# Gathering tokens for eight experts at a time in a mixture-of-experts stage, and loading the eleventh weight block in two transfers

## The chip, the cores and the metric

The kernel runs on one core of one Trainium2 chip. The time is the device time of one execution, in microseconds (us). The core has TensorE (PE, with its weight loads shown as PEld), VectorE (DVE), ScalarE (ACT), GpSimd (POOL) and SyncE (SP), which here only issues loads.

## What is computed

One inference step of a two-layer trunk for 128 context tokens and 128 latent tokens of width 1024, all in float32. Each layer has a mixer (a bidirectional mLSTM with 4 heads of 128, beside grouped-query attention with 8 query and 2 key heads of 64), and then the mixture of experts, the part that the change touches:

```
sel = softmax(xt @ w_router) + b_router            # 16 experts in 4 groups
grp = argmax over groups of (sum of the 2 largest sel in the group)
idx = the 2 largest sel inside that group;  w = scores[idx] / sum(scores[idx])
hid = silu(xt @ w_gate[e]) * (xt @ w_up[e])        # 1024 -> 512, per expert
y   = sum over e of gates[e] * (hid @ w_down[e])   # 512 -> 1024
x   = x + gate * y
```

The weights of one expert are three matrices of 2 MB each, so that one layer's experts are 96 MB (48 transfers of 2 MB), all of which are read.

## The kernel before

Tokens are held transposed, `xT` and `hT` as 8 blocks k of 128 features by 256 tokens. After the router a second copy `htok` holds them with tokens in the partitions, and `pick` (in the tile `lists`) holds for each expert and each of the two token sets (b = 0 context, b = 1 latent) a 0/1 matrix of 128 tokens by 32 places. A **gather** is a matmul of a block of `htok` with `pick`: its result in PSUM has 128 features by the places of several experts. ACT copies it into the tile `xe`, from where it is the stationary operand of the experts' first matmuls. A step for counts above 32 per expert exists, under a branch.

Experts go in 8 **pairs** p, and a quad q is two pairs. For pair p, PE runs `into_hidden(p, 0)` (gate: 16 matmuls of 512 columns) and `into_hidden(p, 1)` (up: 16 more), `turn_hidden` (4 transposes of `hid`, once DVE has made silu(gate) times up) and `down` (32 matmuls). In the even pairs from p = 2 a scatter of the quad before (`scatter_quad`, L1281) stands before and after `turn_hidden`; in pairs 1, 3 and 5 the gather of the next quad stands there: `gather(q + 1, 0, 1)` before `turn_hidden` and `gather(q + 1, 2, 3)` behind it. Pair 0 has `scatter_maps` and `clear_sums` there instead. A float32 matmul leaves two records, so 16 matmuls show as x32.

A quad's gather (L1220) has four PSUM banks, in each two feature blocks k and both b, that is 16 matmuls of 128 columns (4 experts times 32 places).

Weights: SP issues each 2 MB transfer in program order, into 10 **slots** during the experts (7 of the tile `ring`, 2 of `beside`, 1 of `over`). Per pair these are gate in two halves of the features (i = 0, 1), up in two halves (i = 2, 3), and down (i = 4, 5), one slot each. A slot is loaded again when its block has been read, by `expert_read`: i = 0 and 2 by `first_read`, a count that PE raises after the first 8 matmuls of gate or up; i = 1 and 3 when gate or up is done; i = 4 and 5 both when the pair's `down` is done. The transfers are numbered here from 0 within a layer: 0 to 9 go into slots that the mixer leaves, and number 10 (pair 1, i = 4) is the first that needs a slot read by the experts, namely number 0's. Numbers 14 and 15 (pair 2, both halves of up) need the down slots of pair 0. Of the last pair, down comes in halves of 1 MB.

```python
                        if last is not None:
                            was_read(last)
...
                            sp.dma_start(slot_space(slot).rearrange("p (k n) -> p k n", k=KF)[:, 0:n, :],
                                         w[l, 2 * p + i - 4, :, 0:n, :]).then_inc(slot_landed[slot], 16)
```

These are lines 618 to 637 of the program, and `into_hidden` is L1224 to L1240.

## Time and profile before

| | |
|---|---|
| median of 3 runs | 787.18 us (785.57, 787.18, 787.45) |
| the profiled execution | 786.11 us, its span 784.2 us |
| PE busy | 759.6 us, 97% of the span |
| PE weight loads | 410.0 us, 52% |
| DVE, ACT, POOL busy | 356.6, 160.4, 58.2 us |
| transfers | 289.45 MB, mean 369 GB/s |
| TensorE's granted clock, mean | 0.995 of full |

The expert stages are from 197 us (layer 0) and 570 us (layer 1) of the span, each to the next layer or the end. The profiled execution is 1.07 us below the median. In rows of the chain of waits the three fields are start, duration and the work; in rows of stretches each engine's busy time is followed by its count of instructions. Busy time of PE is modelled for pipelined matmuls, so a wait of PE on a transfer is read from the chain, where a DMA stands.

### The profile page before, as it was taken

How to read it: one execution, taken by the hardware profiler on the slowest of the kernel's cores; microseconds unless marked ns; L12 is line 12 of the kernel's file. 1: busy time of each engine (PE TensorE's matmuls, PEld its weight loads, DVE VectorE, ACT ScalarE, POOL GpSimd, SP SyncE). 2: the span in 40 equal slices, each digit the busy share in tenths (PEclk: the TensorE clock that was granted, in tenths of full speed). 3: DMA queues.
4: the chain of work that ended last, by engine and by line, in shares of the span. 5: the costliest groups of instructions: out<-in, count | busy, mean ns of one | idle time of the engine just before them, and what ended most of it. 6: DMA issues, size and time to landing. Idle time of an engine off the chain costs nothing.

```text
span 784.2 us, 11547 instructions
## 1 busy us (share of the span) xinstructions
PE 759.6 (97%) x4960; PEld 410.0 (52%) x4967; DVE 356.6 (45%) x560; ACT 160.4 (20%) x368; POOL 58.2 (7%) x70
## 2 busy tenths in 40 slices
PE   6999999999999999999899999999999999999987
PEld 5655646886434443444245546788643444344424
DVE  0206899786422232132248956788732223213222
ACT  3111224504112111120021111460411211112002
POOL 0410052001100000000010005200110000000000
PEclk8999999999999999999999999999999999999999
DMA  8999699898999999999999970679979999999993
GB/s 313 369 357 409 237 386 410 315 390 327 426 409 427 426 419 424 424 420 425 421 398 401 387 287 8 250 286 393 387 303 399 427 426 419 424 427 417 425 421 148
DMA packets 52980, 289.45 MB, mean 369 GB/s; under 512 B 3448, under 2 KB 5808, under 8 KB 27840
## 3 DMA queue, kind: packets, MB, share of 16 engines
q1 hardware_dynamic: 51200, 285.30, 90.4%
q0 software_dynamic: 1488, 3.31, 1.3%
q8 instruction: 41, 0.67, 0.3%
q10 hardware_dynamic: 240, 0.08, 0.0%
q14 instruction: 11, 0.09, 0.0%
HBM read 286.31 MB, written 2.37 MB: 368 GB/s over the span
## 4 chain that ended last, share of the span: by engine, by line
PE 77%; DMA 12%; DVE 5%; SPq 3%; issue 2%; ACT 1%; POOL 0%; DVEq 0%; ACTq 0%
PE ps L1236 23%; PE ps L879 12%; PE ps L1266 12%; PE ps L1150 7%; DMA ring<-in_w_e_up 5%; PE ps L1220 4%; DMA ring<-in_w_e_down 4%; DMA ring<-in_w_mod 3%; PE ps L897 3%; PE ps L1281 2%; SPq L635 1%; PE ps L727 1%; DVE pT L1860 1%; PE ps L1248 1%; PE ps L1028 1%
## 5 line engine op out<-in xcount | busy, mean ns | idle before, releaser
L1236 PE MATMUL ps<-ring,xe 128*64 128x512 f32 x688 | 151.6, 594 | 4.2 <-DMA ring<-in_w_e_up 4.2
L879 PE MATMUL ps<-ring,hT 128*128 128x512 f32 (+1 forms) x320 | 125.7, 551 | 0.0
L1236 PEld LDWEIGHTS ps<-ring,xe 128*64 128x64 f32 x688 | 48.6, 137 | 105.1 <-issue 100.6
L2205 DVE COPY ye<-ps 64x512 f32<-64x512 f32 (+1 forms) x28 | 19.3, 689 | 163.7 <-PE ps L1266 163.5
L1266 PE MATMUL ps<-ring,exhid 128*32 128x512 f32 x736 | 92.3, 594 | 0.8 <-DMA ring<-in_w_e_down 0.6
L879 PEld LDWEIGHTS ps<-ring,hT 128*128 128x128 f32 x320 | 60.1, 190 | 60.7 <-issue 58.4
L1150 PE MATMUL ps<-hT,ring 128*128 128x256 f32 x256 | 57.1, 381 | 0.0
L2189 DVE RECIPROCAL exhid<-exhid 128x512 f32<-128x512 f32 x16 | 53.6, 3353 | 0.5
L2187 DVE TENSOR_SCALAR exhid<-exhid 128x512 f32<-128x512 f32 x16 | 6.8, 427 | 103.2 <-ACT exhid L1678 103.2
L1266 PEld LDWEIGHTS ps<-ring,exhid 128*32 128x32 f32 x736 | 26.0, 110 | 53.0 <-issue 49.4
L1150 PEld LDWEIGHTS ps<-hT,ring 128*128 128x128 f32 x256 | 48.0, 190 | 7.4 <-issue 1.0
L1236 PE MATMUL ps<-beside,xe 128*64 128x512 f32 x208 | 46.2, 594 | 0.0
L1678 ACT ACTIVATE exhid<-ps 128x512 f32<-128x512 f32 x16 | 9.6, 597 | 144.1 <-PE ps L1236 144.1
L1266 PE MATMUL ps<-beside,exhid 128*32 128x512 f32 x224 | 35.3, 593 | 0.6 <-issue 0.6
L1220 PEld LDWEIGHTS ps<-lists,hT 128*128 128x128 f32 x256 | 29.7, 192 | 6.3 <-issue 6.3
L1220 PE MATMUL ps<-lists,hT 128*128 128x128 f32 x256 | 31.6, 278 | 0.5 <-ACT hT L1657 0.5
L1694 ACT ACTIVATE ye<-ps 64x512 f32<-64x512 f32 (+1 forms) x28 | 16.6, 592 | 68.2 <-PE ps L1266 68.1
L1236 PEld LDWEIGHTS ps<-beside,xe 128*64 128x64 f32 x208 | 14.6, 137 | 30.0 <-issue 29.9
L1671 ACT ACTIVATE xe<-ps 128x512 f32<-128x512 f32 x32 | 19.1, 597 | 54.0 <-PE ps L1220 54.0
L1236 PE MATMUL ps<-over,xe 128*64 128x512 f32 x128 | 28.9, 594 | 0.0
L897 PE MATMUL ps<-hT,ring 128*128 128x256 f32 x128 | 28.8, 381 | 0.0
L1860 DVE SCALAR_TENSOR_TENSOR pT<-ring,cT,pT 128x2048 f32<-128x2048 f32 x12 | 28.2, 2348 | 0.1
(294 smaller groups left out, 867.0 us busy)
## 6 DMA issues: line engine op xcount, KB each, us to landing
ring<-in_w_mod SPq DMA_DIRECT2D x24, 2048.0 KB, 16.8
ring<-in_w_e_up SPq DMA_DIRECT2D x23, 2048.0 KB, 19.9
ring<-in_w_e_gate SPq DMA_DIRECT2D x20, 2048.0 KB, 22.8
ring<-in_w_e_down SPq DMA_DIRECT2D x19, 2048.0 KB, 23.1
beside<-in_w_e_gate SPq DMA_DIRECT2D x8, 2048.0 KB, 22.1
ring<-in_w_in SPq DMA_DIRECT2D x7, 2048.0 KB, 20.4
beside<-in_w_e_down SPq DMA_DIRECT2D x7, 2048.0 KB, 20.3
beside<-in_w_e_up SPq DMA_DIRECT2D x5, 2048.0 KB, 18.6
```

The lines of the kernel that those rows point to most:

```text
L879: mm = pe.matmul(bank[:, 0:width], hT[:, k, b * P:(b + 1) * P], w[:, k, :], start=(k == 0), stop=(k == KD - 1))
L897: mm = pe.matmul(bank[:, j * TOK:(j + 1) * TOK], w[:, k, h * MD:(h + 1) * MD], hT[:, k, :], start=(k == 0 and len(ks) == KD), stop=(k == K ...
L1150: mm = pe.matmul(bank[:, j * TOK:(j + 1) * TOK], w[:, k, c:c + P], cat[:, k, :], start=(k == 0), stop=(k == KD - 1))
L1220: mm = pe.matmul(bank[:, c:c + P], htok[:, b, 2 * i + k, :], pick[:, b, 4 * q:4 * q + 4, :].rearrange("p e c -> p (e c)"), start=True, sto ...
L1236: mm = pe.matmul(bank[PLACES * j:PLACES * j + PLACES, :], xe[:, k, c:c + PLACES], w[:, j, i, :], start=(k == 0), stop=(k == KD - 1))
L1266: mm = pe.matmul(bank[32 * g:32 * g + 32, :], hidT[:, k, c:c + SLOTS], w[j][:, k, half * 512:(half + 1) * 512], start=(k == 0), stop=(k == ...
L1281: pe.matmul(sums(b, dj), ye[:, b, dj * P:(dj + 1) * P], scat[:, q, b * P:(b + 1) * P], start=False, stop=False, skip_group_check=True)
L1671: act.activation(xe[:, 2 * i:2 * i + 2, :].rearrange("p k (e b s) -> p b (k e) s", e=4, b=NB), bank[:, :].rearrange("p (b n s) -> p b n s" ...
L1694: ins = act.activation(ye[r, plane, 0:512], bank[r, :], ACT.Copy)
L1860: ins = dve.scalar_tensor_tensor(modsum[b], w[:, k % 2, :], one, modsum[b], ALU.mult, ALU.add)
L2189: dve.reciprocal(ex[:, :], ex[:, :]).then_inc(silu_step, 1)
L2205: ins = dve.tensor_copy(ye[r, plane, 512:1024], bank[r, :])
```

## The change

1. `gather(h, ...)` serves 8 experts, twice a layer (h = 0 before pair 0, h = 1 in pair 3). Each of its 8 banks holds one feature block k and both b: 2 matmuls of 256 columns. Pairs 1 and 5 have no gather.
2. Its result goes into two tiles, `xe` and the new `small` (8 x 256 floats per partition), by two copies of 256 elements per bank; ACT makes those of even k, DVE those of odd k. Pairs 0, 1, 4, 5 read `xe`, pairs 2, 3, 6, 7 `small`.
3. `small` shares its space with ten small tiles of the mixer (`C0`, `ck`, `cv`, `vx`, `rstd`, `qc`, `qk_r`, `peaks`, `hr`, `nst`). So ACT and DVE wait for `state_out` before the first copy, and two memsets of ones move from the start into each layer.
4. Transfer 10 is split: rows 0 and 2 of each partition once PE has read feature blocks 0 and 1 of gate (a new count `quarter_read`, after 4 matmuls), rows 1 and 3 after `first_read`. `down` of pair 1 waits for both.
5. Bank numbers: the first gather uses 0, 3, 4, 5; `count` goes from bank 5 to 6, ahead of it in DVE's order stand the copies.

```diff
-        put(("count", l), 5)
-        for i, bank in enumerate((0, 3, 1, 2)):
-            put((("gather", 0, i), l), bank)
+        for k in range(KD):
+            put((("gather", 0, k), l), (0, 3, 4, 5)[k % 4])
+        put(("count", l), 6)
...
-            if pair % 2 == 1 and pair < PAIRS - 1:
-                for i in range(4):
-                    put((("gather", pair // 2 + 1, i), l), i % 2)
+            if pair == PAIRS // 2 - 1:
+                for k in range(KD):
+                    put((("gather", 1, k), l), k % 2)
...
+                        if last == ("expert", l, 0, 0):
+                            rows = slot_space(slot).rearrange("p (k n) -> p k n", k=KF)
+                            sp.wait_ge(quarter_read, l + 1)
+                            sp.dma_start(rows[:, 0:KF:2, :], w[l, 2 * p + i - 4, :, 0:KF:2, :]).then_inc(even_rows, 16)
+                            was_read(last)
+                            sp.dma_start(rows[:, 1:KF:2, :], w[l, 2 * p + i - 4, :, 1:KF:2, :]).then_inc(slot_landed[slot], 16)
+                            continue
...
-                def gather(q, *which):
-
-                    for i in which:
-                        bank = begin((("gather", q, i), l))
-                        for k in range(2):
-                            for b in range(NB):
-                                c = b * TOK + k * P
-                                mm = pe.matmul(bank[:, c:c + P], htok[:, b, 2 * i + k, :],
-                                               pick[:, b, 4 * q:4 * q + 4, :].rearrange("p e c -> p (e c)"), start=True, stop=True)
-                        done((("gather", q, i), l), mm)
+                def gather(h, *which):
+
+                    for k in which:
+                        bank = begin((("gather", h, k), l))
+                        for b in range(NB):
+                            mm = pe.matmul(bank[:, b * 2 * P:(b + 1) * 2 * P], htok[:, b, k, :],
+                                           pick[:, b, 8 * h:8 * h + 8, :].rearrange("p e c -> p (e c)"), start=True, stop=True)
+                        done((("gather", h, k), l), mm)
...
-                            if p % 2 == 0 and u == 0 and k % 2 == 0:
-                                taken(pe, (("gather", p // 2, k // 2), l))
+                            if p % 4 == 0 and u == 0:
+                                taken(pe, (("gather", p // 4, k), l))
...
+                            if p == 0 and u == 0 and k == 1:
+                                mm.then_inc(quarter_read, 1)
...
+                    if p == 1:
+                        pe.wait_ge(even_rows, 16 * (l + 1))
...
-                    refill = p % 2 == 1 and q + 1 < QUADS
+                    refill = p == PAIRS // 2 - 1
...
-                        gather(q + 1, 0, 1)
+                        gather(1, 0, 1, 2, 3)
...
-                gather(0, 0, 1, 2, 3)
+                gather(0, *range(KD))
...
+                    for k in which:
+                        key = (("gather", h, k), l)
+                        bank = full(act, key)[:, :].rearrange("p (b q e s) -> p q b e s", b=NB, q=2, e=4)
+                        for q in range(2):
+                            ins = act.activation(places[q][:, k, :].rearrange("p (e b s) -> p b e s", e=4, b=NB), bank[:, q], ACT.Copy)
+                        ins.then_inc(free(key), 1)
...
-                pick_out(0, 0, 1, 2, 3)
+                act.wait_ge(state_out, 16 * STATE_OUTS * (l + 1))
+                pick_out(0, 0, 2, 4, 6)
...
-                chosen(0, 4).then_inc(pick_ready, 1)
+                chosen(0, 8).then_inc(pick_ready, 1)
...
+                dve.wait_ge(state_out, 16 * STATE_OUTS * (l + 1))
+                pick_out(0, 1, 3, 5, 7)
                 modulation_columns(*last_section(l))
```

PE's order from the first gather into pair 0 of layer 0, before (`lists` holds `pick`, `hT` holds `htok`, `rt,ones` is the count, `beside,xe` is gate):

```order
L1220 MATMUL ps<-lists,hT 128x128 [waits bank_read2,bank_read3,bank_read1,bank_read0,pick_ready]
L1220 MATMUL ps<-lists,hT 128x128 x3
L1220 MATMUL ps<-lists,hT 128x128 [waits bank_read3]
L1220 MATMUL ps<-lists,hT 128x128 x3
L1220 MATMUL ps<-lists,hT 128x128 [waits bank_read1]
L1220 MATMUL ps<-lists,hT 128x128 x3
L1220 MATMUL ps<-lists,hT 128x128 [waits bank_read2]
L1220 MATMUL ps<-lists,hT 128x128 x3
L1351 MATMUL ps<-rt,ones 128x16 [waits bank_read5]
L1351 MATMUL ps<-rt,ones 128x16
L1236 MATMUL ps<-beside,xe 64x512 [waits bank_read0,slot_landed7,bank_read1]
```

The same place in the changed kernel, from the fifth of the eight banks on (the first four read the same but for their banks):

```order
L1235 MATMUL ps<-lists,hT 128x256 [waits bank_read0]
L1235 MATMUL ps<-lists,hT 128x256
L1235 MATMUL ps<-lists,hT 128x256 [waits bank_read3]
L1235 MATMUL ps<-lists,hT 128x256
L1235 MATMUL ps<-lists,hT 128x256 [waits bank_read4]
L1235 MATMUL ps<-lists,hT 128x256
L1235 MATMUL ps<-lists,hT 128x256 [waits bank_read5]
L1235 MATMUL ps<-lists,hT 128x256
L1370 MATMUL ps<-rt,ones 128x16 [waits bank_read6]
L1370 MATMUL ps<-rt,ones 128x16
L1251 MATMUL ps<-beside,xe 64x512 [waits bank_read0,slot_landed7,bank_read1]
```

Ahead of pair 0 stand 16 matmuls in both, of 128 columns before and of 256 now.

PE's order in pair 1, from the end of `up` into `down`, before (`exhid` holds `hid`; L1248 is `turn_hidden`):

```order
L1236 MATMUL ps<-ring,xe 64x512 x7
L1220 MATMUL ps<-lists,hT 128x128 [waits bank_read0]
L1220 MATMUL ps<-lists,hT 128x128 x3
L1220 MATMUL ps<-lists,hT 128x128 [waits bank_read1]
L1220 MATMUL ps<-lists,hT 128x128 x3
L1248 MATMUL ps<-cst,exhid 128x128 [waits bank_read3,bank_read2]
L1248 MATMUL ps<-cst,exhid 128x128 x3
L1220 MATMUL ps<-lists,hT 128x128 [waits bank_read0]
L1220 MATMUL ps<-lists,hT 128x128 x3
L1220 MATMUL ps<-lists,hT 128x128 [waits bank_read1]
L1220 MATMUL ps<-lists,hT 128x128 x3
L1266 MATMUL ps<-beside,exhid 32x512 [waits bank_read3,slot_landed8,slot_landed7]
```

And now:

```order
L1251 MATMUL ps<-ring,xe 64x512 x7
L1265 MATMUL ps<-cst,exhid 128x128 [waits bank_read3,bank_read2]
L1265 MATMUL ps<-cst,exhid 128x128 x3
L1285 MATMUL ps<-beside,exhid 32x512 [waits bank_read3,even_rows,slot_landed8,slot_landed7]
L1285 MATMUL ps<-beside,exhid 32x512 x15
```

Nothing stands any more between `up` and `turn_hidden`, and between that and `down`.

SP's order at transfers 10 to 15 of layer 0, before:

```order
L635 DMA beside<-in_w_e_down 128x4096 [waits first_read]
L635 DMA beside<-in_w_e_down 128x4096 [waits bank_full1]
L630 DMA over<-in_w_e_gate 128x2x2048 [waits first_read]
L630 DMA ring<-in_w_e_gate 128x2x2048 [waits bank_full2]
L630 DMA ring<-in_w_e_up 128x2x2048 [waits bank_full2] x2
```

And now:

```order
L633 DMA beside<-in_w_e_down 128x2x1024 [waits quarter_read]
L635 DMA beside<-in_w_e_down 128x2x1024 [waits first_read]
L652 DMA beside<-in_w_e_down 128x4096 [waits bank_full1]
L647 DMA over<-in_w_e_gate 128x2x2048 [waits first_read]
L647 DMA ring<-in_w_e_gate 128x2x2048 [waits bank_full2]
L647 DMA ring<-in_w_e_up 128x2x2048 [waits bank_full2] x2
```

The first row became two; the waits of transfers 11 to 15 are the same.

## Rows read from the trace of the kernel before

**Rows 1.** The page: what the transfers moved, GB/s, in 40 slices of the span.

```profile
GB/s 313 369 357 409 237 386 410 315 390 327 426 409 427 426 419 424 424 420 425 421 398 401 387 287 8 250 286 393 387 303 399 427 426 419 424 427 417 425 421 148
```

**Rows 2.** Stretches: busy time of PE, PEld, DVE, ACT, POOL; PEclk, DMA share, GB/s.

```profile
601.00:770.00 169.00, 166.86 (x1094) 70.21 (x1094) 43.73 (x39) 21.70 (x37) 0.00 (x0) 1.00 1.00 420
760.00:764.00 4.00, 2.78 (x16) 0.96 (x16) 0.72 (x2) 0.00 (x0) 0.00 (x0) 1.00 1.00 418
```

**Rows 3.** The chain of waits, ends of both expert stages: start us, us, what.

```profile
351.07 0.67 SPq L630
351.78 37.76 DMA ring<-in_w_e_up
389.58 3.65 PE ps L1236 x16
...
743.39 28.59 DMA ring<-in_w_e_down
772.03 3.64 PE ps L1266 x32
```

**Rows 4.** The chain of waits, layer 1: gather, pair 0, start of pair 1.

```profile
569.62 3.81 PE ps L1220 x32
573.78 13.88 PE ps L1236 x64
...
590.63 7.07 PE ps L1266 x64
597.71 13.88 PE ps L1236 x64
611.59 1.98 PE ps L1220 x16
614.05 1.79 PE ps L1220 x16
```

**Rows 5.** Timeline of the SP queue: start us, us of a merged row, transfers.

```profile
204.88 3.77 SPq L635 DMA_DIRECT2D beside<-in_w_e_down  x2
...
225.38 0.88 SPq L630 DMA_DIRECT2D ring<-in_w_e_up  x2
...
577.41 0.34 SPq L635 DMA_DIRECT2D ring<-in_w_e_down  x1
...
597.76 0.88 SPq L630 DMA_DIRECT2D ring<-in_w_e_up  x2
```

**Rows 6.** Stretches in and around pair 0, columns as in rows 2.

```profile
577.50:599.20 21.70, 21.64 (x141) 8.12 (x140) 7.30 (x8) 3.14 (x6) 0.00 (x0) 1.00 0.96 387
227.00:228.00 1.00, 1.00 (x8) 0.40 (x6) 0.00 (x0) 0.00 (x0) 0.00 (x0) 1.00 0.83 303
577.00:578.00 1.00, 1.00 (x6) 0.29 (x4) 0.00 (x0) 0.00 (x0) 0.00 (x0) 1.00 0.00 0
578.00:579.00 1.00, 1.00 (x8) 0.38 (x6) 0.00 (x0) 0.00 (x0) 0.00 (x0) 1.00 1.33 229
599.00:600.00 1.00, 1.00 (x8) 0.41 (x6) 0.15 (x1) 0.00 (x0) 0.00 (x0) 1.00 0.59 172
```

**Rows 7.** The chain of waits, layer 0: gather and pair 0.

```profile
197.09 3.81 PE ps L1220 x32
201.25 13.88 PE ps L1236 x64
```

**Rows 8.** The chain of waits: 16 matmuls of 256 columns in layer 0.

```profile
160.78 6.91 PE ps L1150 x32
```

**Rows 9.** Groups by shape: busy us, mean ns of one, idle before.

```profile
L2196 DVE TENSOR_TENSOR exhid<-ps,exhid 128x512 f32<-128x512 f32 x16 | 11.1, 692 | 32.3 <-PE ps L1236 32.3
...
L1688 ACT ACTIVATE exhid<-ps 128x512 f32<-128x512 f32 x16 | 9.5, 595 | 75.3 <-PE ps L1248 75.3
...
L2023 DVE TENSOR_TENSOR qkr<-ps,shares 128x256 f32<-128x256 f32 x8 | 3.4, 425 | 0.3
...
L1624 ACT ACTIVATE qk<-ps 128x258 f32<-128x258 f32 x8 | 3.1, 387 | 1.4 <-PE ps L1120 1.1
```

More of the change, by code:

```diff
@@ L318, in build, with share @@
         m0 = sb("m0", [64, DEPTH, NB])
-        C0 = sb("C0", [P, 2 * MH, MD + 1])
-        ck = sb("ck", [P, NKV * HD])
-        cv = sb("cv", [P, NKV, HD + 1])
-        vx = sb("vx", [P, NB, NKV, HD + 1])
-        rstd = sb("rstd", [P, TOK])
-        qc = sb("qc", [P, NB, 4, 8])
-        qk_r = sb("qk_r", [P, NB, NQ + NKV])
-        peaks = sb("peaks", [P, NB, NQ])
+        small = sb("small", [P, KD * 4 * PLACES])
+        took = [0]
+        def share(n):
+            took[0] += n
+            return small[:, took[0] - n:took[0]]
+        C0 = share(2 * MH * (MD + 1)).rearrange("p (g e) -> p g e", g=2 * MH)
+        ck = share(NKV * HD)
+        cv = share(NKV * (HD + 1)).rearrange("p (g d) -> p g d", g=NKV)
+        vx = share(NB * NKV * (HD + 1)).rearrange("p (b g d) -> p b g d", b=NB, g=NKV)
+        rstd = share(TOK)
+        qc = share(NB * 4 * 8).rearrange("p (b q g) -> p b q g", b=NB, q=4)
+        qk_r = share(NB * (NQ + NKV)).rearrange("p (b h) -> p b h", b=NB)
+        peaks = share(NB * NQ).rearrange("p (b h) -> p b h", b=NB)
+        hr = share(NB * MH).rearrange("p (b h) -> p b h", b=NB)
+        nst = share(P)[0:8, :]
         shares = sb("shares", [P, NB, NQ])
         dn = sb("dn", [P, NB, MH, 2])
-        hr = sb("hr", [P, NB, MH])
-        nst = sb("nst", [8, P])
         mnew = sb("mnew", [64, DEPTH])
@@ L384, in build @@
         sq2 = xe
+        places = (xe, small[:, :].rearrange("p (k c) -> p k c", k=KD))
         h2 = lists
@@ L431, in build @@
         first_read, last_half = sem("first_read"), sem("last_half")
+        quarter_read, even_rows = sem("quarter_read"), sem("even_rows")
         front_in = [sem(f"{g}_front_in") for g in HALVED]
@@ L1210, in _ @@
                 token_rows(3)
[L1211 to L1222 removed]
+                warm((("gather", 0, 2), l), 3)
+                def gather(h, *which):
[5 more added lines that the diff above has]
+                        done((("gather", h, k), l), mm)
                 def into_hidden(p, u):
@@ L1339, in pair @@
                     if refill:
-                        gather(q + 1, 2, 3)
+                        gather(1, 4, 5, 6, 7)
                     if p == 0:
@@ L1665, in _, with pick_out @@
                 token_copy(3)
-                def pick_out(q, *which):
-                    for i in which:
-                        key = (("gather", q, i), l)
-                        bank = full(act, key)
-                        act.activation(xe[:, 2 * i:2 * i + 2, :].rearrange("p k (e b s) -> p b (k e) s", e=4, b=NB),
-                                       bank[:, :].rearrange("p (b n s) -> p b n s", b=NB, n=8), ACT.Copy).then_inc(free(key), 1)
+                def pick_out(h, *which):
+                    for k in which:
[4 more added lines that the diff above has]
+                        ins.then_inc(free(key), 1)
                 def pair(p):
-                    q, a = p // 2, p % 2
-                    refill = a == 1 and q + 1 < QUADS
+                    refill = p == PAIRS // 2 - 1
                     bank = full(act, (("gate", p), l))
@@ L1845, in _ @@
                 dve.memset(mv[:, :, :, MD:MD + 1], 1.0)
+                dve.memset(vx[:, :, :, HD:], 1.0)
+                dve.memset(cv[:, :, HD:], 1.0)
                 def section_sums(l, s, which):
@@ L2171, in _ @@
                 dve.tensor_copy(htok[:, 0, :, 64:128], bank[:, :].rearrange("p (k q) -> p k q", k=KD)).then_inc(free(key), 1)
-                chosen(4, E).then_inc(pick_ready, 1)
+                chosen(8, E).then_inc(pick_ready, 1)
                 step(dve.tensor_tensor(r(R_W), r(R_E), r(R_MASK), ALU.mult))
@@ L2176, in _, with pick_out @@
                 dve.tensor_tensor(beb(R_G), beb(R_W), per_col(r(R_X, 6, 8), E), ALU.mult).then_inc(gates_ready, 1)
+                def pick_out(h, *which):
+                    for k in which:
+                        key = (("gather", h, k), l)
+                        bank = full(dve, key)[:, :].rearrange("p (b q e s) -> p q b e s", b=NB, q=2, e=4)
+                        for q in range(2):
+                            ins = dve.tensor_copy(places[q][:, k, :].rearrange("p (e b s) -> p b e s", e=4, b=NB), bank[:, q])
+                        ins.then_inc(free(key), 1)
+                dve.wait_ge(state_out, 16 * STATE_OUTS * (l + 1))
+                pick_out(0, 1, 3, 5, 7)
                 modulation_columns(*last_section(l))
@@ L2201, in pair @@
                             dve.tensor_copy(scat[:, i, :], bank[:, 0:TOK]).then_inc(free(key), 1)
+                    if refill:
+                        pick_out(1, 1, 3, 5, 7)
                     key = (("down", p, 1), l)
```

10 lines of the change are left out of this document (4 added, 6 removed).

## The prediction

> **What bounds the kernel now.** I read the page first. PE is busy 97% of the span, but the rate row says more: through both expert stages the transfers hold 417 to 427 GB/s in nearly every slice [rows 1], and no other slice is above that. In layer 1 from 601 to 770 the DMA share is 1.00 at 420 GB/s [rows 2], 5.0 us per 2 MB. The chain of waits then says what ends each stage: in layer 0 the last `up` block, which landed at 389.58 after 37.76 us in a full queue, in layer 1 the last half of `down`, landed at 772.0 and issued 28.6 us before [rows 3]. PE is close behind. Pair 5 of layer 0 ends at 351.07 [rows 3]; one pair is 25.1 us (13.88 of gate and up, 4.25 of gather and turn, 7.0 of down, as in pair 1 of layer 1: 611.59 less 597.71, 615.84 less 611.59, and a down like the one at 590.63 [rows 4]), so PE alone would end pair 7's `up` at 351.07 + 25.1 + 13.9 = 390.1. It ends at 389.58 + 3.65 = 393.2 [rows 3]. PE waits some 3.1 us for weights in the last pair.
>
> So an expert stage is one stream of transfers, which runs full from transfer 14 on. **What decides its end is when it starts and what it idles at the start.** Around pair 0 of layer 1 [rows 4 to 6]: all ten slots are full, the stream stops (0 GB/s at 577), PE starts pair 0 at 573.78, has read the first block 8 matmuls later (3.47 us), SP issues transfer 10 at 577.41, and data flows from 578 on. Transfers 10 to 13 are 8.4 MB, and 21.7 us at 387 GB/s from 577.5 to 599.2 are 8.4 MB: they end at 599.2. Transfers 14 and 15 wait for the end of pair 0's `down` at 597.71, are issued at 597.76, and data comes some 1.5 us later: the microsecond from 599 has 172 GB/s. That is a small gap, and it shows that **the stream is here tied to PE's `down` of pair 0**. In layer 0 the gather starts at 197.09, pair 0 at 201.25 [rows 7], transfer 10 is issued at 204.88 with data still in the queue, and transfer 14 at 225.38 [rows 5]; the microsecond from 227 dips to 303 GB/s [rows 6]: the same tie, with next to no gap.
>
> **The first gather.** Before: 16 matmuls of 128 columns in 3.81 us, then the count, pair 0 starts 4.16 us after the gather [rows 4]. After: 16 matmuls of 256 columns. The trace has just this shape, 128 rows by 128 columns of weights with 256 columns moving: 16 of them in 6.91 us [rows 8]. Bounds: not under 3.81 (as if columns were free), not over 7.62 (two old gathers). I take 6.91, the same shape. **Pair 0 starts 3.10 us later, in each layer.** Can the start of the gather move? It waits for ACT's last token copy; DVE's `chosen` makes 8 experts in place of 4 before its own token copy, some 0.27 us more going by 425 ns for 256 elements and 692 for 512 [rows 9], which ends before ACT's copy does. The copies out of PSUM keep up: a bank takes PE 0.86 us, ACT two copies of about 387 ns and DVE two of about 425 ns [rows 9], and each has every second bank. The wait for `state_out` is long met, POOL itself has waited for it before the router.
>
> **The refills.** A quad's gather in pair 1, 3 or 5 is 1.98 + 1.79 = 3.77 us [rows 4]. It goes in pairs 1 and 5, but it covered two waits that now stand bare: `turn_hidden` needs DVE's last product (692 ns), `down` needs ACT's copy (595 ns) [rows 9], each with some 0.2 us of signalling (an estimate, by the 0.16 us from the first block's read at 577.25 to SP's issue). Of 4.25 us between `up` and `down` some 2.4 stay (0.9 wait, 0.5 to 0.7 turn, 0.8 wait), so each pair gains 1.9. Pair 3 gets 6.91 in place of 3.77, and two banks that alternate, with a wait of up to 0.5 us in all: +3.6. PE over six pairs: +3.1 - 1.9 + 3.6 - 1.9 = +2.9 us. So PE does not come earlier to the last pair; it arrives about as late as the weights do, and its wait there stays near 3 us. In pair 3 the late slots cost the stream nothing: after transfer 14 it falls behind PE by 30 - 25 = 5 us a pair.
>
> **Transfer 10 in two parts.** PE raises `quarter_read` after 4 matmuls in place of 8, 1.74 us sooner. Issue in layer 1: 577.41 + 3.10 - 1.74 = 578.8, so 1.4 us later than now, not 3.1. The second MB is issued 1.74 us after, while the first still takes 2.5. Transfers 10 to 13 then end near 600.6. But transfer 14 waits for `down`, which ends at 597.71 + 3.10 = 600.81, data near 602.5. The stream has a gap of about 1.9 us before it, and what the split won is lost there. In layer 0 transfer 10 comes 0.4 to 1 us late, 13 ends near 227.7, transfer 14's data 3.1 later than now, near 230.3. Whether two transfers of 1 MB run a little slower than one of 2 is therefore free up to 1.9 us. SP issues one transfer more (0.34 us [rows 5]) and nothing is queued behind it that is ready. `down` of pair 1 waits for both parts, which land long before it.
>
> **Sum.** The stream is 3.1 us late from transfer 14 on, in each layer, and has no slack to catch up: 2 x 3.1 = **+6.2 us**. The mixer of layer 1 starts with the end of layer 0 and moves with it. The moved memsets are two of a few elements a layer on DVE, which there waits for weights. Profiled execution: 786.1 + 6.2 = 792.3. The median of the runs shown is 1.1 above it, their mean 0.6. I forecast **793.0**, its own range 791 to 795.
>
> **Rivals.** (a) *The head start carries.* If the stream is not tied to `down` (the dips at 599 and 227 being only the start of a transfer), only transfer 10 counts: +1.4 in layer 1, +0.5 in layer 0, and PE's +2.9 falls into its wait of 3.1. +1.9 us: 788 to 789. Against it: 14 and 15 stand in SP's order with a wait for `down`, and with no data left in the queue at 599.2. The Trainium skill speaks for it: Perfetto Trace Analysis, "DMA Optimizations", says that splitting a transfer may let parts start sooner and the whole end sooner where the engines are idle. They are idle here, so by that rule the split pays. The trace agrees for transfer 10 alone, since the bytes behind it wait for another event. Chance 0.08.
>
> (b) *The wide gather costs no more than the old one* (the side that is not slower). If 16 matmuls of 256 columns took 3.8 to 4.5 us, pair 0 would start less than 0.7 us late, `down` of pair 0 with it, and the stream's end would move by 0 to 1.4 us over both layers: 787.2 to 788.6; it decides at 5.0 us, where twice the delay reaches 2.4. Only with the lost refills and an earlier stream could it be faster, which the tie to `down` forbids: at most -1 us. For it stands the Trainium skill's Perfetto Trace Analysis, "Matmuls", that larger matmuls are more efficient than smaller ones. By the rows 128 columns take 3.81/16 = 238 ns and 256 take 432 ns, 9% less per column: the rule holds, but a gather of 8 experts ahead of pair 0 is still 3.1 us longer. Chance 0.05.
>
> (c) *Worse than the sum.* PE now has bare waits in pairs 1 and 5 as well as in pair 7. If it idles so that the granted clock falls to the lower level before the last `down`, what stands behind the last transfer (3.64 + 1.1 us and the closing transposes and scatter) doubles: some +4 in a layer, 795 to 799. Against it: at 760 to 764 PE is busy 2.78 of 4 us with the clock at 1.00 [rows 2]. A gather in pair 3 that blocks on its two banks would come on PE's side alone, where up to 0.2 us are free: +1 to 2. Chance 0.09.
>
> **How the numbers follow.** The forecast has 0.78. A measurement of this kernel can tell about 0.3%, 2.4 us, from no change: over 789.5 is slower. Slower: forecast and (c) 0.87, less 0.02 for the edge toward 789.5: 0.85. Same: (a), (b) and that edge: 0.12. Faster: 0.03. The range is 789.5 to 796: it holds the forecast with the bounds of the gather (7.62 in place of 6.91 would add 1.4) and the spread of the runs (1.9), and the lower half of (c); it leaves out (a), most of (b) and the rest of (c).
>
> **What would show it.** In the profile after: the gather of 16 matmuls at 6.9 us in the chain, pair 0 4.16 + 3.1 = 7.26 us behind its start; in layer 1 the stop of the stream about 1.4 us longer, and a second gap of about 2 us after transfer 13; a full stream from there; PE waits of about 0.9 us before the turn in pairs 1 and 5; both stages ended by a transfer, the last landing about 3 us later after the gather's start than now (202.4 us in layer 1). Wrong, if that landing comes less than 2 us later, if a stage ends on PE with no wait on a transfer in pair 7, or if the mixer's time changes by more than 1 us.

## The result and the profile after

| | before | after |
|---|---|---|
| median | 787.09 us (4 runs) | 798.02 us (797.36, 797.98, 798.06, 801.12) |
| profiled execution, span | 786.11, 784.2 | 797.36, 795.4 |
| PE busy | 759.6, 97% | 763.2, 96% |
| transfers | 289.45 MB, 369 GB/s | 289.43 MB, 364 GB/s |

The changed kernel takes 1.015 times as long [1.0121, 1.018]: slower, by 10.9 us between the medians and 11.25 between the profiled executions. The forecast was slower by about 6, in a range of 789.5 to 796. The direction held, the size did not.

The page of after, its rate in 40 slices, to be read against [rows 1]:

```profile
GB/s 315 367 362 411 214 404 413 319 382 335 360 400 427 425 419 424 423 420 425 421 400 399 349 261 1 240 292 370 402 238 397 427 424 422 422 427 417 425 421 155
```

Both plateaus stand as before. What differs is ahead of each: 360 and 400 in slices 11 and 12 where 426 and 409 stood, and 238 and 397 in slices 30 and 31 where 303 and 399 stood.

The chain of waits of after, first gather and pair 0 in both layers (start us, us, what; L1235 is the gather, L1251 gate and up, L1285 `down`):

```profile
197.33 7.14 PE ps L1235 x32
204.82 13.88 PE ps L1251 x64
...
577.52 7.15 PE ps L1235 x32
585.01 13.88 PE ps L1251 x64
```

The gather takes 7.15 us in place of 3.81, and pair 0 starts 7.49 us behind the gather's start in place of 4.16 [rows 4, 7], 3.33 later in each layer. Everything in pair 0 follows by as much.

The chain of after, ends of both expert stages, against [rows 3]:

```profile
357.07 35.60 DMA ring<-in_w_e_up
...
392.72 3.65 PE ps L1251 x16
...
399.23 7.07 PE ps L1285 x64
406.30 3.40 issue
409.70 3.60 PE ps L1310 x31
...
413.33 1.14 DVE xT L1856 x4
...
735.40 37.95 DMA ring<-in_w_e_up
...
773.40 3.65 PE ps L1251 x16
...
779.92 7.02 PE ps L1285 x64
786.94 1.10 PE ps L1310 x15
```

And the same of before, the part that was not shown:

```profile
396.10 7.13 PE ps L1266 x64
403.23 1.10 PE ps L1291 x15
...
404.36 2.17 DVE xT L1837 x8
...
775.67 1.10 PE ps L1291 x15
```

In both layers the chain now waits for the last `up` block (before, layer 1 waited for the last half of `down`). That block is there 195.39 and 195.88 us behind the gather's start, where it was there after 192.49 and 191.71: 2.9 and 4.2 us later, so the stream is late by about what the forecast said, or somewhat more. Counted in the same way, the last `down` ends at 208.97 and 209.42 us, where it ended at 206.14 and 206.05: +2.83 and +3.37. But behind the last `down` of layer 0 stands something new: **PE executes nothing for 3.40 us** with no wait that the profile shows, and the scatter (L1310) that follows then lasts 3.60 us. From the end of `down` to the end of DVE's copies it is 414.47 - 406.30 = 8.17 us, before 406.53 - 403.23 = 3.30: +4.87. A stretch behind the stop (columns as in [rows 2]):

```profile
410.00:412.00 2.00, 2.00 (x21) 2.00 (x20) 0.19 (x1) 0.00 (x0) 0.00 (x0) 0.50 1.00 394
```

The waits of PE in after, in total, times, longest:

```profile
PE ps L1285 <- ACT exhid L1708: 3.6, 4, 0.9
PE ps L1310 <- issue: 3.4, 1, 3.4
PE ps L1265 <- DVE exhid L2230: 3.2, 4, 0.8
PE ps L1251 <- DMA ring<-in_w_e_up: 2.6, 3, 1.2
```

The first and third are the bare waits in pairs 1 and 5 (two layers, so four times), 0.8 to 0.9 us each. The second is the stop. Of the fourth, 0.5 us fall in layer 0 and 2.1 in layer 1, where before had 2.1 in each.

The bare waits had a second effect. Behind those of pair 1 in layer 0 PE's granted clock fell to 0.50, and `down` took 8.77 us in place of 7.07:

```profile
245.21 8.77 PE ps L1285 x64
```

```profile
246.00:248.00 2.00, 2.00 (x12) 0.54 (x8) 0.00 (x0) 0.00 (x0) 0.00 (x0) 0.50 1.04 442
```

The profiles of the six kernels with the wide gather (after, e1, e3, e7, e8, e9 below) have 24 such pairs between them, and five of these show this fall, each of 1.70 us: one in after, one in e1, two in e3, one in e8. In before and in the other runs, where pairs 1 and 5 have the old gather, no pair shows it. It did not end a stage in after, since PE still waited 0.53 us for the last `up` block of layer 0, but it took most of what PE had to spare there.

SP's queue in layer 1 of after, against [rows 5], and the rate behind it:

```profile
586.92 0.58 SPq L633 DMA_DIRECT2D ring<-in_w_e_down  x1
588.64 0.54 SPq L635 DMA_DIRECT2D ring<-in_w_e_down  x1
...
608.99 1.20 SPq L647 DMA_DIRECT2D ring<-in_w_e_up  x2
```

```profile
590.00:592.00 2.00, 2.00 (x12) 0.71 (x10) 0.00 (x0) 0.00 (x0) 0.00 (x0) 1.00 0.97 297
592.00:594.00 2.00, 2.00 (x12) 0.58 (x10) 1.26 (x2) 0.60 (x1) 0.00 (x0) 1.00 0.95 326
594.00:596.00 2.00, 2.00 (x12) 0.72 (x10) 2.00 (x1) 0.00 (x0) 0.00 (x0) 1.00 1.08 350
...
610.00:612.00 2.00, 2.00 (x12) 0.65 (x10) 0.39 (x1) 0.00 (x0) 0.00 (x0) 1.00 0.81 238
```

Two things are to be seen. There is a second gap before transfer 14's data, at 610 to 612. And **the two halves of transfer 10 come slowly**: for some 6 us the DMA engines are busy all the time (share 0.95 to 1.08) but move 297 to 350 GB/s, where the kernel before had 401 to 451 at this point of pair 0.

So three causes were to be told apart: the wide gather ahead of pair 0, the slow halves, and the stop.

### The profile page after: what moved, and what is told of

The parts are those of the page before. It is cut to its first block, busy times and chain, and to the rows that moved or that the text cites. A ratio compares the mean times of both kernels' runs of the same rounds, so it can differ in the third digit from the quotient of the medians.

```text
span 795.4 us, 11334 instructions
## 1 busy us (share of the span) xinstructions
PE 763.2 (96%) x4839; PEld 407.6 (51%) x4839; DVE 368.0 (46%) x594; ACT 152.1 (19%) x368; POOL 58.2 (7%) x70
## 2 busy tenths in 40 slices
DMA packets 53779, 289.43 MB, mean 364 GB/s; under 512 B 3480, under 2 KB 5840, under 8 KB 28896
## 4 chain that ended last, share of the span: by engine, by line
PE 76%; DMA 13%; DVE 5%; issue 3%; SPq 1%; ACT 1%; POOL 0%; DVEq 0%; ACTq 0%
PE ps L1251 22%; PE ps L1285 13%; PE ps L896 12%; DMA ring<-in_w_e_up 9%; PE ps L1167 7%; PE ps L1235 4%; DMA ring<-in_w_mod 3%; PE ps L914 3%; PE ps L1300 2%; PE ps L1310 1%; PE ps L1265 1%; PE ps L744 1%; DVE pT L1881 1%; PE ps L1045 1%; SPq L601 1%
## 5 line engine op out<-in xcount | busy, mean ns | idle before, releaser
L1285 PE MATMUL ps<-ring,exhid 128*32 128x512 f32 x736 | 92.0, 594 | 3.4 <-ACT exhid L1708 2.7
L1251 PE MATMUL ps<-ring,small 128*64 128x512 f32 x368 | 81.0, 594 | 2.6 <-DMA ring<-in_w_e_up 2.6
L1251 PE MATMUL ps<-ring,xe 128*64 128x512 f32 x320 | 70.3, 594 | 0.0
L1285 PEld LDWEIGHTS ps<-ring,exhid 128*32 128x32 f32 x736 | 27.6, 110 | 54.0 <-issue 51.8
L1251 PEld LDWEIGHTS ps<-ring,small 128*64 128x64 f32 x368 | 26.0, 137 | 56.9 <-issue 53.4
L1251 PEld LDWEIGHTS ps<-ring,xe 128*64 128x64 f32 x320 | 22.5, 137 | 46.5 <-issue 46.4
L1285 PE MATMUL ps<-beside,exhid 128*32 128x512 f32 x224 | 37.0, 627 | 0.9 <-ACT exhid L1708 0.9
L1698 ACT ACTIVATE exhid<-ps 128x512 f32<-128x512 f32 x16 | 9.6, 597 | 145.7 <-PE ps L1251 145.7
L1235 PE MATMUL ps<-lists,hT 128*128 128x256 f32 x128 | 30.0, 388 | 0.5 <-ACT hT L1676 0.5
L1708 ACT ACTIVATE exhid<-ps 128x512 f32<-128x512 f32 x16 | 9.6, 597 | 106.1 <-PE ps L1265 106.1
L1251 PE MATMUL ps<-beside,xe 128*64 128x512 f32 x128 | 28.2, 594 | 0.0
L1881 DVE SCALAR_TENSOR_TENSOR pT<-ring,cT,pT 128x2048 f32<-128x2048 f32 x12 | 28.1, 2345 | 0.1
L1881 DVE SCALAR_TENSOR_TENSOR sideways<-ring,cT,sideways 128x2048 f32<-128x2048 f32 x12 | 28.1, 2344 | 0.0
```

Of the source, the lines that this page charges most:

```text
L1235: mm = pe.matmul(bank[:, b * 2 * P:(b + 1) * 2 * P], htok[:, b, k, :], pick[:, b, 8 * h:8 * h + 8, :].rearrange("p e c -> p (e c)"), start ...
L1251: mm = pe.matmul(bank[PLACES * j:PLACES * j + PLACES, :], places[p // 2 % 2][:, k, c:c + PLACES], w[:, j, i, :], start=(k == 0), stop=(k = ...
L1285: mm = pe.matmul(bank[32 * g:32 * g + 32, :], hidT[:, k, c:c + SLOTS], w[j][:, k, half * 512:(half + 1) * 512], start=(k == 0), stop=(k == ...
L1698: act.activation(ex[:, :], bank[:, :], ACT.Exp, scale=-1.0).then_inc(silu_exp, 1)
L1881: ins = dve.scalar_tensor_tensor(modsum[b], w[:, k % 2, :], one, modsum[b], ALU.mult, ALU.add)
```

## The experiments

Ratios are to runs of the kernel before on the same chip, with 95% intervals; 0.1% is 0.8 us. "Before" had medians of 786.02 (beside e1 to e4), 786.41 (e5, e7, e8, e9) and 786.43 us (e6, e10, e11, e12). A difference between two experiments is less sure than either ratio: by the intervals, it is known to some 2 us where the runs are few.

| run | median us | ratio |
|---|---|---|
| e1_unsplit | 794.82 | 1.0114 [1.0097, 1.0131] |
| e2_split_alone | 786.95 | 1.0014 [1.0004, 1.0024] |
| e3_after_more_warm | 794.01 | 1.0096 [1.0078, 1.0113] |
| e4_before_less_warm | 789.74 | 1.0052 [1.0035, 1.0068] |
| e5_late_pair0 | 792.90 | 1.0072 [1.0049, 1.0094] |
| e7_unsplit_more_warm | 792.26 | 1.0067 [1.0043, 1.0091] |
| e8_halves_in_a_row | 791.07 | 1.006 [1.0041, 1.008] |
| e9_even_odd_together | 793.78 | 1.0085 [1.0061, 1.0109] |
| e6_late_pair2 | 787.80 | 1.0012 [1.0001, 1.0022] |
| e10_gather_in_two_down_halves | 783.98 | 0.9962 [0.9949, 0.9975] |
| e11_gather_in_two | 786.25 | 0.9998 [0.9989, 1.0007] |
| e12_down_halves | 784.68 | 0.9982 [0.997, 0.9993] |

### The split: e1, e2

e1 is the changed kernel with transfer 10 in one piece:

```diff
-                        if last == ("expert", l, 0, 0):
...
-                            continue
...
-                            if p == 0 and u == 0 and k == 1:
-                                mm.then_inc(quarter_read, 1)
...
-                    if p == 1:
-                        pe.wait_ge(even_rows, 16 * (l + 1))
```

> The changed kernel with transfer 10 in one piece again, after first_read. Theory A (the stream is tied to the end of pair 0's down): within 0.5 us of the changed kernel's 798.0, since the head start is lost before transfer 14; transfer 10 is issued 1.7 us later, transfers 14 and 15 at the same time. Rival (the head start counts): slower than the changed kernel by 1.4 to 2 us in layer 1 and up to 0.5 us in layer 0. Third possibility: faster by 1 us or more, if the two parts of 1 MB, which moved at some 310 GB/s, cost more than they win.

Measured: 794.82 us, 3.2 below the changed kernel by medians, 2.8 by the ratios. The third possibility came, and not the 0.5 us of theory A: the split costs time. The stream behind transfer 10 ran at 434, 426 and 442 GB/s in stretches of 2 us. But e1 still had a stop in layer 0, of 2.58 us, so the two kernels did not differ by the split alone. From the end of `down` to the end of the scatter it is 5.28 us in e1 and 7.00 in after, so that 1.7 of the 3 us belong to the stop and only some 1.2 are left for the split.

e2 is the kernel before with the same lines added and nothing else.

> The kernel before with only transfer 10 in two parts. Theory A: the same as before, 787.1, within 0.7 us. Rival: faster by 1.5 to 2 us (1.7 in layer 1). If the parts' slower rate (some 310 GB/s instead of 420) is paid on the path: up to 1 us slower.

Measured: 786.95 us, +0.14%, or 1.1 us (0.3 to 1.9), the price that was expected for slow halves on the path. Its first stretches with data in layer 1 show 295, 287, 381 and 338 GB/s. The head start of 1.7 us brought nothing here either.

### The stop: e3, e4

The stop is put down to "issue", and stands where PE jumps over the step for counts above 32: `with pe.If(limit[0] > SLOTS)` (L1414), behind the last `down` and ahead of `scatter_pair`. The branch is in both kernels. These two runs only move PE's program against itself, with warm-up matmuls at the very start, which change nothing in the result. e3 is the changed kernel, e4 the one before:

```diff
-            warm(("x", 0), 95, 64)
+            warm(("x", 0), 147, 64)
```

```diff
-            warm(("x", 0), 95, 64)
+            warm(("x", 0), 31, 64)
```

> The changed kernel with 52 more warming matmuls of 64 columns at the start, where PE waits for its inputs anyway. They move all later PE instructions on by 104 places, near where the kernel before had them in layer 0. Theory B (the stop of 3.40 us in front of the last scatter of layer 0, which nothing in the profile releases, is PE fetching instructions behind the branch around the overflow step, and hangs on where that branch lies): the stop is gone or has another length, and the time is 793 to 794.5. Rival (the stop comes from the change's own order: banks, semaphores, waits): stop of 3.4 us and 798 as before.

> The kernel before with 64 warming matmuls fewer at the start (31 in place of 95), which moves all later PE instructions up by 128 places, about as far as the change does in layer 0. Theory B: a stop of about 3.4 us appears in front of the last scatter of layer 0, and the time is 790 to 792. Rival: no stop, 787 to 788 (the first matmuls at the lower clock may cost some tenths).

The same place in the chain of e3, then of e4:

```profile
399.86 7.07 PE ps L1285 x64
406.93 1.10 PE ps L1310 x15
```

```profile
395.80 7.07 PE ps L1266 x64
402.87 3.45 issue
406.32 1.17 PE ps L1291 x15
```

With 52 matmuls more at the start the changed kernel has no stop in layer 0, one of 0.86 us in layer 1 where it had none, and is 0.54% or 4.2 us nearer to before. With 64 fewer the kernel before has one, of the same length, and a short one of 1.16 us at the same place of layer 1, and is 4.1 us slower by the ratio (789.74 us, just under the 790 to 792 expected). So the stop belongs to the position of instructions at the branch, not to the gather or to the split. That it is the fetch of instructions is an inference, and the rows for it are mixed. In after, the transfers between 406.30 and 409.70 hold one packet of the instruction queue, and e4's between 402.87 and 406.32 too:

```profile
q8 instruction: 1, 0.02, 1.9%
```

But e1's stop of 2.58 us (405.27 to 407.85) holds none, and neither does e4's short one in layer 1; and the kernel before, which has no stop, has none in the first 1.2 us behind `down` but one between 405 and 406.6. The packets alone decide nothing. The Trainium skill's Runtime: NRT & Kernel Launch, "Instruction fetch mechanics", says that a taken branch to a page of 256 instructions that has not been fetched must wait for a fetch. The trace agrees in that a stop stands at this branch and goes or comes with the position (3.45 us in e4, none in before); that it is a fetch is not shown. Which pages PE held was not seen.

### The gather and the shape of the halves: e7, e8, e9

All three are the changed kernel with 147 warm-up matmuls, so without the long stop (e7 has 0.90 us and e8 0.68 us in layer 1, e9 none). e7 has transfer 10 in one piece. e8 and e9 have it in two that are issued together after `first_read`, with no head start: e8 rows 0, 1 and then 2, 3 of each partition, e9 rows 0, 2 and then 1, 3.

```diff
                             rows = slot_space(slot).rearrange("p (k n) -> p k n", k=KF)
-                            sp.wait_ge(quarter_read, l + 1)
...
                             was_read(last)
-                            sp.dma_start(rows[:, 1:KF:2, :], w[l, 2 * p + i - 4, :, 1:KF:2, :]).then_inc(slot_landed[slot], 16)
+                            sp.dma_start(rows[:, 0:2, :], w[l, 2 * p + i - 4, :, 0:2, :]).then_inc(even_rows, 16)
+                            sp.dma_start(rows[:, 2:KF, :], w[l, 2 * p + i - 4, :, 2:KF, :]).then_inc(slot_landed[slot], 16)
```

> The changed kernel with transfer 10 in one piece and 52 more warming matmuls at the start, that is the wide gather alone, without the stop behind the branch. Theory A as corrected (wide gather ahead of pair 0 moves the stream 2.9 to 3.1 us a layer; the split costs 1.1 us a layer more; the stop 3.4 us plus a slow clock behind it): 791.3 to 792.3, no stop of over 1.2 us, the last up block of layer 1 landing about 194.7 us after the start of its gather. Rival (the unsplit kernel was faster only because its stop was shorter): 793.5 to 794.5, as with the split and more warming.

> As the changed kernel with more warming, transfer 10 in two transfers of 1 MB, but rows 0 and 1 and then rows 2 and 3 of each partition (8 KB at a stretch), both after first_read. Theory C (the rate falls because rows 0 and 2 are fetched in pieces of 4 KB): full rate, about 425 GB/s, from the first 2 us of data on, time 791.3 to 792.5 as unsplit. Rival (two transfers in place of one are slow in themselves): some 320 GB/s for 8 us, 793.5 or more.

> As the run with halves in a row, but rows 0 and 2 and then rows 1 and 3, both issued after first_read. Theory C: some 320 GB/s for 8 us of data, and with no head start left 794.5 to 796.5, slower than the changed kernel with more warming (794.0). Rival (the rate falls because the second part comes 1.7 us behind the first): full rate, 791.3 to 792.5.

e7: 792.26 us, +0.67%. This is the wide gather with what it does to the refills, and next to nothing else: **+5.3 us** (3.4 to 7.2) with that short stop in it, where the forecast had 6.2. e8 is the same within the intervals (+4.7; at 791.07 us it is 0.2 under the range expected), e9 is 2.7 us above e8 by medians (2.0 by the ratios), and would be 3.4 above it without e8's short stop. It is not above e3 (794.01), which has the head start, so the 794.5 to 796.5 expected of e9 did not come. Same bytes, same count of transfers, same moment of issue: what differs is that e8's halves are pieces of 8 KB that follow each other in a partition, and e9's are pieces of 4 KB that skip every second row. Transfers from 580 to 592 us, e8 then e9:

```profile
DMA packets 368, 3.41 MB, mean 284 GB/s; under 512 B 32, under 2 KB 32, under 8 KB 32
...
ring<-in_w_e_down SPq DMA_DIRECT2D x2, 1024.0 KB, 5.8
```

```profile
DMA packets 556, 2.36 MB, mean 197 GB/s; under 512 B 28, under 2 KB 28, under 8 KB 540
...
ring<-in_w_e_down SPq DMA_DIRECT2D x2, 1024.0 KB, 7.6
```

e9's halves are 512 packets under 8 KB and land 7.6 us after issue in place of 5.8. Each also occupied SP for some 0.6 us (0.58 and 0.61) where e8's took 0.34 and 0.43. In the first four stretches of 2 us with data e8 moved 258, 442, 463 and 410 GB/s, e9 168, 264, 309 and 471: 0.7 MB less, 1.7 us of a full stream in each layer. e9 then has no gap before transfer 14 (422 GB/s where e8 shows 266), which gives back 0.7.

Part of e9's loss in its trace is something else. In layer 1 PE waited 2.7 us for the last `up` block, the granted clock fell, and that block took 5.35 us in place of 3.65:

```profile
768.59 5.35 PE ps L1250 x16
```

```profile
769.00:771.00 2.00, 2.00 (x7) 0.50 (x5) 0.00 (x0) 0.00 (x0) 0.00 (x0) 0.50 1.01 422
```

So 1.70 us of this execution are the clock's; whether the other three have them is not known. And e8, with the slow clock in pair 1 of layer 1, ends that layer on PE with no wait for a transfer in pair 7.

Is it the length of the pieces? The kernel before speaks against that as the whole cause. In the mixer of layer 1, from 448 to 454 us, its loads go in pieces of 3.3 KB on average, at 405 GB/s:

```profile
DMA packets 741, 2.43 MB, mean 405 GB/s; under 512 B 20, under 2 KB 20, under 8 KB 741
```

The pattern, two transfers that each skip every second row, was not run apart from the length. Halves of adjacent rows keep the rate, halves of alternate rows do not; why is open.

### Is the stream tied to pair 0: e5, e6

e5 is the kernel before with 15 warm-up matmuls of 512 columns put between the first gather and pair 0, and 15 fewer at the start. e6 puts the same 15 ahead of pair 2.

```diff
+                warm((("gate", 0), l), 15)
                 for p in range(PAIRS):
```

```diff
+                    if p == 2:
+                        warm((("gate", 2), l), 15)
```

> The kernel before with 15 warming matmuls of 512 columns (about 3.2 us of PE) between the first gather and pair 0 of each layer, and 15 fewer at the start. Theory A: the delay alone, without a wide gather, costs what the wide gather does: both streams land about 3 us later, 791.5 to 792.5 against 786.0. Rival (PE's last-pair wait of 3.1 us takes it up, and the rest of the change's loss is in the copies or the refills): under 788.

> The kernel before, with 15 warm-up matmuls of 512 columns (3.2 us in the run that had them ahead of pair 0) moved from the start of the kernel to a place ahead of pair 2, in each layer. It is the same delay on PE as in the run before pair 0, two pairs later. Theory A (only what delays pair 0's down delays the stream of transfers; later PE has about 3 us to spare against the last landing): the last up block lands as long after the gather as in the kernel before (192.5 us in layer 0, within 1), PE's wait for it in pair 7 goes from about 3 us to near 0, and the time is 786 to 789. Rival (any delay of PE in the stage costs its length, since every slot is freed by PE): 2 x 3.2 = 6.4 us more, near 793.

Both show 3.23 us of PE more per layer:

```profile
577.13 3.23 PE ps L793 x14
```

```profile
251.14 3.23 PE ps L793 x14
```

The first is e5, the second e6. Ahead of pair 0 they cost 6.5 us by medians, the full 2 x 3.2 (5.7 by the ratio, 3.9 to 7.4; 792.90 us is 0.4 above the range expected), with the old gather, no split and no stop. Ahead of pair 2 they cost 1.4 us by medians, 0.9 by the ratio. In e6 PE's wait for `up` nearly goes, its last `up` of layer 0 is there 193.4 us behind the gather in place of 192.5, and layer 1 ends on PE, but its last `down` ends 206.04 us behind the gather, where it ended at 206.05 before: there the whole 3.23 us was to spare. The waits of PE, first e5, then e6:

```profile
PE ps L1236 <- DMA ring<-in_w_e_up: 4.0, 4, 1.2
```

```profile
PE ps L1236 <- DMA ring<-in_w_e_up: 0.4, 1, 0.4
```

The theory came out, the rival (6.4 us for any delay) did not. What the stage loses is decided in pair 0, as long as later delays stay under the 3 us or so that PE has to spare.

### A head start, and a stream that starts earlier: e10, e11, e12

If the stream is tied to pair 0's `down`, a head start of transfer 10 is worth nothing and an earlier transfer 14 is worth all of itself. e11 is the kernel before with its first gather in two (and other banks for its second part); e12 has pair 0's `down` written with k outside, and transfers 14 and 15 loaded as halves (in pieces of 8 KB), the first after half of `down`; e10 is both.

```diff
-                gather(0, 0, 1, 2, 3)
+                gather(0, 0, 1)
...
+                        if p == 0 and u == 0 and part == 1:
+                            gather(0, 2, 3)
```

```diff
+                        if last == ("expert", l, 0, 4):
+                            for j in range(2):
+                                if j == 0:
+                                    sp.wait_ge(half_read, l + 1)
+                                else:
+                                    was_read(last)
...
+                            if k == 1:
+                                mm.then_inc(half_read, 1)
```

> The kernel before, with the first gather in two alone: two banks, the first gate block of pair 0, then the other two banks. Pair 0 starts 1.9 us sooner after the gather, its down ends when it did. Theory A (the stream is tied to pair 0's down): transfer 10 is issued sooner and the gap ahead of transfer 14 grows by as much; the time stays, 786.5 to 787.5. Rival (the head start of transfer 10 carries to the end, which was rival (a) of the prediction): 1.9 us a layer at most, 783 to 785.

> The kernel before, with transfers 14 and 15 alone loaded as halves of 1 MB, the first halves after half of pair 0's down. Theory A: the gap ahead of transfer 14 (in layer 1 some 1.5 us at half the rate) goes and the last up block lands 0.5 to 1 us sooner in layer 1, 0 to 0.5 in layer 0: 785.5 to 786.8. Rival (the gap is the start of a transfer and costs nothing, or the smaller transfers cost as much as they win): 787 to 788.

> The kernel before, with the first gather in two (two banks, the first gate block of pair 0, the other two banks), and with pair 0's down written so that the first half of both down slots is free after half of it: transfers 14 and 15 are loaded as halves of 1 MB in pieces of 8 KB, the first halves some 3.5 us earlier. Theory A (the end of each stage is the end of one stream of transfers that is tied to pair 0's down, with a gap ahead of transfer 14): the gap goes and the last up block lands 1 to 2.5 us sooner after the gather, in layer 1 more than in layer 0: 783 to 786. Rival (the stream is bound by its rate alone, what is gained early is lost in a later wait of the queue): 786.5 to 787.5, no difference from before.

SP's queue and the stretches behind pair 0 in layer 1: e11, e12, e10.

```profile
575.10 0.34 SPq L635 DMA_DIRECT2D ring<-in_w_e_down  x1
...
597.71 0.88 SPq L630 DMA_DIRECT2D ring<-in_w_e_up  x2
```

```profile
597.10:599.10 2.00, 2.00 (x16) 0.63 (x10) 1.37 (x2) 0.00 (x0) 0.00 (x0) 1.00 0.59 123
```

```profile
593.88 4.24 SPq L629 DMA_DIRECT2D ring<-in_w_e_up  x4
```

```profile
597.17:599.17 2.00, 2.00 (x14) 0.77 (x12) 1.38 (x2) 0.48 (x1) 0.00 (x0) 1.00 0.99 414
```

```profile
597.38:599.38 2.00, 2.00 (x16) 0.63 (x10) 1.37 (x2) 0.94 (x2) 0.00 (x0) 1.00 1.00 418
```

In e11 transfer 10 is issued 1.8 us sooner behind the gather (575.10 - 569.10 = 6.0 us, before 577.41 - 569.62 = 7.8), transfer 14 half a microsecond later (28.6 in place of 28.1 us), and the stream falls to 123 GB/s ahead of it, in a stretch where the kernel before has 340. The time does not move: 0.9998 [0.9989, 1.0007]. This is the head start of the change in its cleanest form. It brought nothing; at the most it made good the half microsecond by which transfer 14 is late, and not the 1.9 us a layer of the rival. In e12 the halves are issued from 593.88, the gap is gone and the time falls by 0.18%, 1.4 us (1.8 by medians), a little more than the expectation gave. In e10 both are there: the gap stays closed although transfer 10 is early, and it takes 783.98 us, 0.38% below before, 14 us below the changed kernel, and the fastest kernel of this study.

## Why the prediction was right and wrong

**The step that failed** is the end of the sum. The stream was to be 3.1 us late in each layer and everything else to move with it ("2 x 3.1 = +6.2 us. The mixer of layer 1 starts with the end of layer 0 and moves with it"). Two things stood beside these 6.2 us: a stop of PE behind layer 0's last `down`, which the sum did not have (+4.87 us in the trace, about +4 by e3 and e4), and a price of the split that it put at nothing (+1.1 us by e2, up to some 3 by the others). The signs that the prediction named for being wrong all stayed quiet, since none of them looked at the place between the last `down` and the mixer.

**What bounds the stage**: right. "The stream is here tied to PE's `down` of pair 0" is what e5, e6 and e11 show, each from another side. Rival (a), the head start that carries, is refuted in its size by e11. The rule of the Trainium skill's Perfetto Trace Analysis, "DMA Optimizations", that speaks for splitting held for e12 (-0.18%), where the part that starts sooner is the one that others wait for, and failed for the change (e2: +0.14%).

**The first gather**: right in kind, 0.24 us short a layer. 7.15 us against 6.91 taken, pair 0 behind it by 3.33 against 3.10. The mixer of layer 0 has four runs of this shape in the chain, at 7.06, 6.91, 7.10 and 7.10 us, and the prediction took the shortest. The whole price by e7 is 5.3 us (3.4 to 7.2), 4.4 without its short stop, against 6.2. Rival (b) falls with it.

**The refills and the bare waits**: right in pairs 1 and 5, short in the rest. Between `up` and `down` 2.40 us stay there, as written, in waits of 0.8 and 0.9 us and the turn. But pair 3's gather took 3.90 + 3.71 = 7.61 us in place of 6.91, pairs 1 and 5 gained 1.74 each in place of 1.9, and one fall of the clock took 1.70. By the end of pair 5 PE was later by 5.35 us in layer 0 and by 3.70 in layer 1, where +2.9 was forecast, and its wait in pair 7 did not stay near 3 us: 0.5 of 2.1 us is left in layer 0. PE's slack of 3.1 us a layer was about right (e6: all 3.23 us in layer 1, 2.4 of them in layer 0). So the change came close to a second bound, PE itself, that the prediction thought 3 us away.

**The mixer of layer 1**: right, -0.04 us.

**Transfer 10 in two parts**: two statements, one right, one wrong. The head start is lost before transfer 14, as said, and the second gap is there. But "whether two transfers of 1 MB run a little slower than one of 2 is therefore free up to 1.9 us" is **a term that failed**. Halves of rows 0, 2 and 1, 3 ran at 297 to 350 GB/s for some 6 us, in e9 a loss of 1.7 us of stream in a layer, of which 0.7 comes back ahead of transfer 14. The term was taken as nothing and is +1 to +3 us: 1.1 by e2, 2.3 by the ratios between e3 and e7 (1.8 by medians), 2.7 by medians between e9 and e8, of which up to 1.7 may be the slow clock. The bounds should have held it: the prediction has no row for a transfer in two parts, so the rate was unknown.

Where the changed kernel loses it is open, for there the head start does cover the slow halves. From 10 to 34 us behind the gather of layer 1 it moved as much as e7, which has no split, and fell back only in the 6 us behind that, after the gap. First after, then e7:

```profile
587.52:611.52 24.00, 23.99 (x154) 8.84 (x152) 7.29 (x8) 3.14 (x6) 0.00 (x0) 1.00 0.95 358
611.52:617.52 6.00, 6.00 (x32) 2.00 (x30) 0.85 (x2) 0.60 (x1) 0.00 (x0) 1.00 0.98 392
```

```profile
582.57:606.57 24.00, 23.91 (x153) 8.83 (x152) 7.29 (x8) 3.15 (x6) 0.00 (x0) 1.00 0.90 359
606.57:612.57 6.00, 6.00 (x31) 2.00 (x29) 0.84 (x2) 0.60 (x1) 0.00 (x0) 1.00 1.00 416
```

**The sum**: the stop is the larger part of the miss, 3.40 us and the slow clock behind it, +4.87 in the trace and about +4 in the runs (4.2 between after and e3, and 4.1 for e4, each with a short stop of about 1 us in layer 1). It was in no rival. Rival (c) had a clock at the lower level and a time of 795 to 799, but from idle waits in the stage. Such falls did come behind the bare waits, one of them in after, and took 1.70 us each, but in after it was hidden behind the last `up` block; what counted was the fall behind the stop, where PE idled for no wait at all. That 798.0 lies inside (c)'s 795 to 799 is luck.

With the three prices from the runs, 5.3 + 1 to 3 + 4, the sum is 10 to 12 us, against 10.9 measured. Taken as e7, e3 less e7 and after less e3, the three add up by construction; e2 and e4 are apart from that, and give 5.3 + 1.1 + 4.1 = 10.5. The split of the first two inside a single trace is less sure: the stages of after are 6.2 us longer together (2.83 + 3.37), and those of e7 and e3 are 5.1 and 7.2, so one execution differs from the next by about 1 us.

## What to carry to other kernels

Where a stage is a stream of transfers behind a first event, find the last event that a transfer of that stream waits for. Work moved ahead of it costs its full length; work behind it is free up to what the engine has to spare; and a transfer before it that starts sooner gains little or nothing. When a transfer is split, give each part adjacent rows: here that kept the rate, and alternate rows did not.

A difference between two builds that stands at a taken branch, with PE idle for no reason that the profile names, may belong to where the code lies. Run either kernel with a few dozen harmless instructions more and fewer at its start, before the change is given the blame or the credit.

## What the runs showed of the hardware

- A jump of PE over a block that isn't executed cost nothing that could be seen in the kernel before and in e3, 2.58 us in e1, 3.40 and 3.45 us in after and e4, and 0.7 to 1.2 us in layer 1 of e3, e4, e7 and e8. Between after and e3, and between before and e4, only the position of the instructions differs. In after and in e1 PE's clock was at 0.50 behind it; in e4, with a stop of the same length, the scatter took 1.17 us as without one, so the slow clock doesn't always follow.
- Loads of 1 MB that take every second row of 4 KB kept the DMA engines busy (0.95 to 1.08) at some 300 GB/s in after; the same megabyte as adjacent rows, in pieces of 8 KB, ran at 442 and 463 GB/s in e8. Issuing one took SP 0.6 us in place of 0.34 to 0.43. Short pieces alone did not do it: pieces of 3.3 KB on average ran at 405 GB/s in before.
- Two waits of PE of 0.8 and 0.9 us, with 0.7 us of work between them, were followed by a granted clock of 0.50 in 5 of 24 cases, and the `down` behind them took 8.77 to 8.80 us in place of 7.07.
- 16 matmuls of 256 columns that fill eight banks took 7.14 us, against 6.91 to 7.10 for the same count and shape in the mixer.
